# Two-layer hybrid decoder trunk: seven block products in the FFN's gate/up groups, and other step tables at the DeltaNet's edges

## The reference

```
h = h + gated_deltanet(rms_norm(h))       # layer 0: 16 q/k heads, 32 v heads of 128, chunks of 64
h = h + (silu(x @ Wg) * (x @ Wu)) @ Wd    # FFN, x = rms_norm(h), hidden width 5632
kv = shared_kv(rms_norm(h))               # projected, block-compressed once
h = h + nsa_attention(rms_norm(h), kv)    # layer 1
h = h + (silu(x @ Wg) * (x @ Wu)) @ Wd    # second FFN
out = rms_norm(h)
```

## Time and profile before

| | |
|---|---|
| runs | 2955.64, 2954.94, 2952.25 us, median 2954.94 |
| profiled execution | 2950.0 us, its span 2948.2 us |
| TensorE busy | 2823.6 us, 96%, 13696 matmuls |
| VectorE busy | 1800.2 us, 61% |
| ScalarE busy | 1497.7 us, 51% |
| DMA | 493.02 MB, mean 167 GB/s |
| granted TensorE clock | mean 0.986 of full |

### The profile page before, as it was taken

How to read it: one execution, slowest core, us unless ns; L and a number is a source line. 1 busy time by engine, 2 the same in 40 slices (tenths; PEclk the granted TensorE clock), 3 DMA queues, 4 the chain that set the end, 5 groups by cost and what they waited for, 6 DMA issues and landing times.

```text
span 2948.2 us, 39238 instructions
## 1 busy us (share of the span) xinstructions
PE 2823.6 (96%) x13696; PEld 2342.0 (79%) x13696; DVE 1800.2 (61%) x2183; ACT 1497.7 (51%) x1978; POOL 30.2 (1%) x29
## 2 busy tenths in 40 slices
PE   7989999999988999999999999799989999999997
PEld 6778887887866788888888878688878888888886
DVE  5767877877876555555555554556664555555555
ACT  6676767677664444444444444454444444444443
POOL 0000000000000000000000000000000000000000
PEclk9999999999998999999999999899999999999999
DMA  6434444444433555555555555533336555565553
GB/s 239 153 122 150 154 157 147 162 138 159 159 114 97 168 185 193 192 190 190 190 185 190 193 176 190 174 119 111 107 126 209 185 188 193 188 195 190 191 192 129
DMA packets 135079, 493.02 MB, mean 167 GB/s; under 512 B 15008, under 2 KB 15328, under 8 KB 134624
## 3 DMA queue, kind: packets, MB, share of 16 engines
q1 hardware_dynamic: 133776, 487.82, 50.1%
q10 hardware_dynamic: 1232, 4.23, 0.4%
HBM read 489.86 MB, written 2.13 MB: 167 GB/s over the span
## 4 chain that ended last, share of the span: by engine, by line
issue 56%; PE 40%; DVE 1%; DMA 1%; ACT 1%; POOL 0%; POOLq 0%; ACTq 0%; SPq 0%; DVEq 0%
PE ACC L527 12%; PE ACC L529 12%; PE ACC L528 12%; PE SIDE L535 1%; DMA RAW<-stream 1%; DVE W_LO L1258 1%; PE SIDE L854 0%; PE SIDE L828 0%; ACT W_HI L909 0%; PE SIDE L851 0%; PE SIDE L833 0%; PE SIDE L838 0%; PE SIDE L866 0%; DVE H L1283 0%; ACT WORK L914 0%
## 5 line engine op out<-in xcount | busy, mean ns | idle before, releaser
L1258 DVE TENSOR_TENSOR W_LO<-RAW,W_HI 128x1024 fp32r<-128x1024 f32 x912 | 1100.5, 1222 | 767.9 <-ACT W_HI L909 764.2
L909 ACT ACTIVATE W_HI<-RAW 128x1024 fp32r<-128x1024 f32 x912 | 959.7, 1059 | 1008.0 <-PE ACC L529 983.4
L527 PE MATMUL ACC<-W_HI,X_HI 128*128 128x512 f32 x2496 | 990.2, 397 | 16.9 <-DVE W_LO L1258 12.5
L528 PE MATMUL ACC<-W_LO,X_HI 128*128 128x512 f32 x2496 | 975.7, 391 | 0.0
L529 PE MATMUL ACC<-W_HI,X_LO 128*128 128x512 f32 x2496 | 975.5, 391 | 0.0
L527 PEld LDWEIGHTS ACC<-W_HI,X_HI 128*128 128x128 f32 x2496 | 471.2, 189 | 112.1 <-issue 18.0
L529 PEld LDWEIGHTS ACC<-W_HI,X_LO 128*128 128x128 f32 x2496 | 470.7, 189 | 99.7
L528 PEld LDWEIGHTS ACC<-W_LO,X_HI 128*128 128x128 f32 x2496 | 471.4, 189 | 93.0 <-issue 0.5
L527 PE MATMUL ACC<-W_HI,A_HI 128*128 128x512 f32 x1024 | 410.2, 401 | 13.1 <-issue 10.4
L529 PE MATMUL ACC<-W_HI,A_LO 128*128 128x512 f32 x1024 | 403.0, 394 | 0.0
L528 PE MATMUL ACC<-W_LO,A_HI 128*128 128x512 f32 x1024 | 402.3, 393 | 0.0
(11 more groups left out here) (247 smaller groups left out, 1688.8 us busy)
## 6 DMA issues: line engine op xcount, KB each, us to landing
RAW<-stream SPq DMA_DIRECT2D x912, 512.0 KB, 3.9
WORK<-gdn_rows ACTq DMA_DIRECT2D x8, 512.0 KB, 4.2
WORK<-xt SPq DMA_DIRECT2D x4, 512.0 KB, 9.3
H<-x SPq DMA_DIRECT2D x2, 1024.0 KB, 13.3
out<-WORK SPq DMA_DIRECT2D x4, 512.0 KB, 3.9
WORK<-tails SPq DMA_DIRECT2D x2, 512.0 KB, 11.1
WORK<-gfin SPq DMA_DIRECT2D x1, 1024.0 KB, 8.3
K<-consts SPq DMA_DIRECT2D x1, 518.0 KB, 6.7
```

The source lines that it names most:

```text
L527: nc.tensor.matmul(dst, hi[:, at:at + P], wh, start=first and h % 2 == 0 and q == 0, stop=False)
L528: nc.tensor.matmul(dst, hi[:, at:at + P], wl, start=False, stop=False)
L909: nc.scalar.activation(W_HI[:, h % WS, :], raw_piece(h), ACT.Copy).then_inc(hi_ready, 1)
L1258: nc.vector.tensor_tensor(W_LO[:, h % WS, :], raw_piece(h), W_HI[:, h % WS, :].bitcast(f32), SUB).then_inc(lo_ready, 1)
```

## The change

**FFN.** In groups 1 to 10, half of the contraction of gate and up (every other pair of 128-row blocks) goes by a Strassen-Winograd scheme: with tokens in two blocks and columns in two, seven block products of sums take the place of eight. In each quarter j of a group six operations follow one another: `11`, `21`, `13`, `24` (the seven products), `pa`, `pb` (the other pair of blocks, ordinarily). `21` is half as wide. `13` and `24` multiply sums of weight blocks, which VectorE forms from RAW (`weight_sum`: t13 of 1024, t24 in two halves) and which are then split like a piece; they come from no DMA. Sums of token blocks are formed once per FFN (`token_sums`). A column group holds 256 columns each of gate and up. Four products go to the ACC tiles and are mixed by VectorE (`c_add`), the rest are accumulated in SIDE; `c_sum` adds both up. The transposes of the hidden activations stand before the last two down pieces, go through a copy in SBUF (`hid_t`), and A_HI and A_LO are made from that. Group 10 is written out beside the loop. SP frees RAW by a list (`RAW_FREE`).

**DeltaNet.** Iterations 0, 1, 7, 8 and 9 get piece lists of their own; four output pieces move from 7 to 8 (`old4` to `old7`). Tables for 0, 1, 7 and 8 and the one of the loop are new. Accumulators alternate over the written-out iterations. The activations of group 6 go to another buffer, B_HI and B_LO.

```diff
+FFN_PIECE = {"11": 0, "21": 1, "13": 0, "24": 0, "pa": 2, "pb": 3}
+FFN_ORDER = 4 * ["11 21 13 24 pa pb"]
+FFN_OPS = [(kind, j, 4 * j + FFN_PIECE[kind]) for j in range(4) for kind in FFN_ORDER[j].split()] +     [("d", n, 16 + n) for n in range(8)]
+FFN_AT = {op[:2]: e for e, op in enumerate(FFN_OPS)}
+RAW_FREE = [FFN_AT[kind, j] for j in range(4) for kind in ("11", "21", "pa", "pb")] + [24 + n for n in range(8)]
+MORE = 8 * (FBLK - 1)
...
+PIECES_0 = "qk 0 1 2 3 4 6 7 8 v 9 10 11 12 13 14 15 16 z 17 18 20 21 23 25 27 29"
+PIECES_1 = "qk 0 1 2 3 4 5 6 7 v 8 9 10 11 12 13 14 15 z 16 18 20 22 25 28 29 30"
+PIECES_7 = "qk 0 1 2 3 4 5 6 7 v 8 9 10 11 12 13 14 16 out 18 20 25 30"
+PIECES_8 = "old4 0 1 2 3 z 4 5 6 8 9 10 11 12 out 13 14 15 16 18 19 20 26"
+PIECES_9 = "out 0 1 2 3 4 5 6 7"
...
+def gdn_accs():
+    accs, turn = {}, 0
+    for it in sorted(GDN_PIECES):
+        slots = gdn_slots(it)
+        if it == LATE_Z:
+            turn = 0
+        for part, n in (slots[hs] for hs in sorted(slots)):
+            if n == 0 or (part in ("out", "old") and n % 2 == 0):
+                turn = 1 - turn
+            accs[it, part, n] = turn
+    return accs
...
 LAST_STEPS = gdn_table(SOLVE, """
-    0 y0
-    1 t0 u0
-    2 conv_v0a y1
-    3 t1 u1 conv_v0b
-    4 y2 strict
-    5 t2 u2 conv_v1a
-    7 y3
-    8 t3 u3 conv_v1b silu_v y4
+    0 y0 t0 u0 conv_v0a
+    2 y1 t1 u1 conv_v0b
+    3 y2 strict
+    4 t2 u2 conv_v1a
+    6 y3
+    7 t3 u3 conv_v1b silu_v
+    8 y4
     9 t4 u4
-    10 y5 v_t2
-    11 t5 u5
-    12 nw
+    10 v_t2 y5
+    11 t5
+    12 u5 nw
     13 ru
-    14 v0
-    15 s ks
+    14 v0 s
+    15 ks
     16 v1 o
-    19 osum oscale
+    18 osum oscale
     20 o_t""")
...
 FIRST_STEPS = gdn_table(ONCE, """
     8 gates1
     10 gates1b
     13 gates2""") + gdn_table(PREP, """
-    9 qk_t conv_qk0a conv_qk0b
-    10 conv_qk1a
+    8 qk_t conv_qk0a conv_qk0b
+    9 conv_qk1a
     11 conv_qk1b
-    15 silu_qk squares
-    17 ss fill qkn factors
-    20 k_t dif v_t
-    21 beta decay kkqk qk1 nr init masks""")
+    12 silu_qk
+    14 squares
+    17 ss fill factors qkn
+    20 v_t dif k_t
+    21 beta kkqk decay
+    22 qk1 nr init
+    23 masks""")
...
+        def gdn_act(g):
+            return (B_HI, B_LO) if isinstance(g, int) and g == GROUPS - 2 else (A_HI, A_LO)
...
+        def three(dst, hi, lo, wh, wl, start, stop):
+            nc.tensor.matmul(dst, hi, wh, start=start, stop=False)
+            nc.tensor.matmul(dst, hi, wl, start=False, stop=False)
+            return nc.tensor.matmul(dst, lo, wh, start=False, stop=stop)
+        def up_products(pe, c, e):
+            kind, j, _ = FFN_OPS[e]
+            pe.wait_ge(lo_ready, c + (e + 1))
+            m1, m6, m7, m5 = (ACC[i][:, k * COLS:(k + 1) * COLS] for i in range(2) for k in range(2))
+            c11, c12, c21, c22 = (SIDE[1 - i][:, k * COLS:(k + 1) * COLS] for i in range(2) for k in range(2))
+            kt = 4 * j + (2 if kind[0] == "p" else 0)
+            a11, a21, a12, a22 = (tuple(b[:, at:at + P] for b in (X_HI, X_LO))
+                                  for at in ((kt + q) * SEQ + t * P for q in range(2) for t in range(NT)))
+            z5, z7, z6, z3 = (tuple(b[i][:, k * COLS + j * P:k * COLS + (j + 1) * P] for b in (Z_HI, Z_LO))
+                              for i in range(2) for k in range(2))
+            f, l = j == 0, j == 3
+            early = f and FFN_AT["pa", 0] < FFN_AT["24", 0]
+            todo = {"11": [(m1, a11, 0, f, l), (c12, z3, 1, f, False)],
+                    "21": [(c11, a12, 0, f, False)],
+                    "13": [(m5, z5, 0, f, l), (m7, z7, 1, f, l)],
+                    "24": [(m6, z6, 0, f, l), (c21, a22, 1, f and not early, False)],
+                    "pa": [(c11, a11, 0, False, False), (c21, a21, 0, early, False), (c12, a12, 1, False, False),
+                           (c22, a22, 1, f, False)],
+                    "pb": [(c12, a11, 0, False, l), (c22, a21, 0, False, l), (c11, a12, 1, False, l),
+                           (c21, a22, 1, False, l)]}[kind]
+            for dst, (hi, lo), half, start, stop in todo:
+                wh, wl = (b[:, e % WS, half * COLS:(half + 1) * COLS] for b in (W_HI, W_LO))
+                m = three(dst, hi, lo, wh, wl, start, stop)
+            m.then_inc(w_used, 1)
...
+            for e in range(0 if first or final_ else 24):
+                if e == 0:
+                    pe.wait_ge(acc_out[0], ph.before("m16", it))
+                if e == FFN_AT["24", 0] or FFN_OPS[e][0] == "pa" and e < FFN_AT["24", 0]:
+                    pe.wait_ge(side_out[0], ph.before("hid_t", it))
+                if e == FFN_AT["13", 0]:
+                    pe.wait_ge(acc_out[1], ph.before("m57", it))
+                up_products(pe, c, e)
+            for k in range(0 if first else 4):
+                pe.wait_ge(acc_out[k % 2], ph.before(f"down{k}", it))
+                if k == 0:
+                    pe.wait_ge(act_lo, it + (FBLK if ph is FFN1 else 0))
+                if k == 3 and not final_:
+                    pe.wait_ge(hid_done, it + (FBLK - 1 if ph is FFN1 else 0))
+                    turn(by_block(hid), 0)
+                for half in range(2):
...
+        def ffn_hi(act, ph, base, ob, it, e):
+            (kind, j, piece), wrap = ffn_ahead(it, e)
+            act.wait_ge(w_used, ffn_c(ob, it) + (e + 1 - WS))
+            dst = W_HI[:, e % WS, :]
+            if kind in ("13", "24"):
+                act.wait_ge(t_done, sums_done(ph, it, wrap) + (3 * j + (1 if kind == "13" else 3)))
+                src = t13 if kind == "13" else t24
+            else:
+                act.wait_ge(raw_full[piece % RAWS], (ffn_raw(base, it) + 24 * wrap) * (16 // RAWS) + 16 * (piece // RAWS + 1))
+                src = raw_piece(piece)
+                if kind == "21":
+                    dst, src = dst[:, 0:COLS], src[:, COLS:2 * COLS]
+            nc.scalar.activation(dst, src, ACT.Copy).then_inc(hi_ready, 1)
...
+                if k == 3 and not final_:
+                    take_out(act, 0, ph.after("hid_t", it), hid_t)
...
+                act.wait_ge(w_used, c + (16 if first else 32))
+                act.wait_ge(side_out[0], ph.after("hid_t", it))
+                nc.scalar.activation(A_HI[:, :], hid_t, ACT.Copy).then_inc(act_hi, 1)
...
+        def ffn_lo(dve, ph, base, ob, it, e):
+            (kind, j, piece), wrap = ffn_ahead(it, e)
+            dve.wait_ge(hi_ready, ffn_c(ob, it) + (e + 1))
+            hi, lo = W_HI[:, e % WS, :].bitcast(f32), W_LO[:, e % WS, :]
+            if kind == "21":
+                nc.vector.tensor_tensor(lo[:, 0:COLS], raw_piece(piece)[:, COLS:2 * COLS], hi[:, 0:COLS],
+                                        SUB).then_inc(lo_ready, 1)
+            else:
+                src = {"13": t13, "24": t24}.get(kind, raw_piece(piece))
+                nc.vector.tensor_tensor(lo, src, hi, SUB).then_inc(lo_ready, 1)
+            for n in range(3):
+                weight_sum(dve, ph, base, ob, it, e + 2 - n, n)
+        def weight_sum(dve, ph, base, ob, it, e, n):
+            (kind, j, piece), wrap = ffn_ahead(it, e)
+            if kind != "11":
+                return
+            b11_22, b12_21 = raw_piece(piece), raw_piece(piece + 1)
+            done = sums_done(ph, it, wrap) + 3 * j
+            if n < 2:
+                dve.wait_ge(lo_ready, ffn_c(ob, it) + (e - 3 + n))
+            if n == 0:
+                for p in (piece, piece + 1):
+                    dve.wait_ge(raw_full[p % RAWS], (ffn_raw(base, it) + 24 * wrap) * (16 // RAWS) + 16 * (p // RAWS + 1))
+                i = nc.vector.tensor_tensor(tiles2(t13), tiles2(b11_22),
+                                            b12_21[:, 0:COLS].unsqueeze(1).broadcast_to([P, 2, COLS]), ADD)
+            else:
+                dve.wait_ge(t_done, done + n)
+                a = (t13 if n == 1 else t24)[:, 0:COLS]
+                b = (b11_22 if n == 1 else b12_21)[:, COLS:2 * COLS]
+                i = nc.vector.tensor_tensor(t24[:, (n - 1) * COLS:n * COLS], a, b, ADD)
+            i.then_inc(t_done, 1)
...
+            def hid_lo():
+                dve.wait_ge(act_hi, it + hi0)
+                nc.vector.tensor_tensor(A_LO[:, :], hid_t, A_HI[:, :].bitcast(f32), SUB).then_inc(act_lo, 1)
+            if final_:
+                hid_lo()
+            for e in range(0 if first or final_ else 24):
+                if e == 20:
+                    hid_lo()
+                if e == 22:
+                    dve.wait_ge(w_used, c + 22)
+                    dve.wait_ge(m1_out, it + late)
+                    nc.vector.tensor_tensor(dif, ACC[0][:, COLS:2 * COLS], c_add[:, 0:COLS], SUB).then_inc(acc_out[0], 1)
+                ffn_lo(dve, ph, base, ob, it, e + WS)
+                if e == 22:
+                    m7, m5 = ACC[1][:, 0:COLS], ACC[1][:, COLS:2 * COLS]
+                    dve.wait_ge(acc_out[0], ph.after("m16", it))
```

(25 more changed lines are left out.)

496 lines of the change are left out of this document (336 added, 160 removed).

## The result

The changed kernel takes 2915.03 us (median of 4 runs, 2910.82 to 2917.91) against 2953.6 for the kernel before beside it: ratio 0.9871, 95% interval 0.9853 to 0.9889. It is faster by 38.6 us where 84.7 was forecast, and it lies above the range, whose end was 2904. The direction was right, and the size less than half.

A forecast was written before the change was run, and what follows sets the result against it. TensorE, busy 2823.6 of 2948.2 us, was taken as the bound. Terms -54.3 + 2 - 2.8 - 11.6 - 18.0 = -84.7 us, from a median of 2954.94, gave 2870.2 us; range 2854 to 2904.

The forecast's parts named there:

- The failed step: FFN, t13's wait for raw 21: 4.7 to 6.2 us allowed, landing 3.5 to 5.4, so it fits; called most exposed.
- Rival C: FFN: t13 waits for raw 21 and stops VectorE and TensorE; decides from landings of 7.3 us, 3030 at 8.2; chance 0.04.
- -54.3 for 240 matmuls: Both FFNs: 12 fewer matmuls in each of 20 groups, at 0.2263 us each, save 54.3 us if TensorE stays the limit.
- VectorE, +2: FFN group starts, where slack is thinnest at 0.6 us: 0.1 us charged for each of 20 groups, bounds 0 to 20.
- rival A: FFN: VectorE, at 90% load, runs late and delays TensorE; half the FFN gain goes, 2897 us; chance 0.15.
- The last block, -2.8: End of each FFN: transposes before the last two products cut the wait from 4.9 to about 3.5; -2.8 us for both.
- Iterations 0 and 1, -11.6: First DeltaNet iterations: alternating accumulators and moved steps remove waits and half-rate loss, 14.6 us named, 3 given back.
- Iterations 2 to 6, 0: Middle DeltaNet iterations: a few steps move by a slot; no change expected, between -5 and +5 us.
- Iterations 7 to 9, -18.0: Last DeltaNet iterations: -8.5 idling in 8, -4.2 at the seam to 9, +2 in 7, -7.3 clock.
- This only moves work: Four output pieces, 10.9 us of products, go from DeltaNet iteration 7 to 8 with no gain or loss of their own.
- About 5.5 of idling in place of 14.0: DeltaNet iteration 8: changed waits, with direct steps y1 to t1 and y0 to t0 at 1.7 us each, give -8.5 us.
- -7.3 for the clock: DeltaNet iterations 7 to 9: of about 11 us lost at half rate, two thirds go with the waits.

The follow-up runs named there:

- t13 later: Changed kernel with VectorE's weight sum t13 issued one place later, behind the low part of pb instead of ahead of it: 2884.55 us.
- the run with the operation inside the loop: Kernel with t13 later plus one useless 512-wide VectorE operation per quarter, ahead of the low part of 21: 2887.89 us.
- The run that took it away: Kernel with t13 later, ks moved to slot 21 in iteration 1 and a piece between ks and v1 in iterations 1 and 7: 2885.71 us.
- the one without the wait: Changed kernel with t13 and t24 formed from raw piece pb, so no early wait for raw 21; part of the computation left out: 2885.38 us.

## Why the prediction was wrong in size

**The failed step, 32 us by the stages and 30.5 by the medians: "4.7 to 6.2 us. Landing takes 3.5 to 5.4, median 3.9. It fits".** The places were laid out rightly, the comparison was wrong. The allowance of 6.2 is had once: a t13 that starts late also frees raw 21 late. What must fit into every turn is all that lies between two t13s: 5.3 us of VectorE, 0.2 to ask, the landing, 0.1 to start. At 10.2 that leaves 4.6 for a landing, and 3.9 is a median of requests spread evenly. Bunched as the new order bunches them they take 5.5. The prediction named this wait as the one most exposed and noted that pieces would be asked for in pairs, but let only landings above 6.2 cost anything. Rival C had the right mechanism and a wrong point of decision: from 4.6 on it costs, not from 6.2.

**-54.3 for 240 matmuls.** Held but for 8 us: with no wait left a group takes 63.9, not 63.5. In a steady group with t13 later (1141 to 1205 us) the matmuls that take a sum of token blocks, and those next to them, start 229 to 241 ns apart where others start 227 apart. That makes 0.37 of the 0.4; why they do isn't shown. Each FFN's first group takes 46.9 where it took 46.3. In all, the FFNs of the kernel with t13 later give 46.2 of the 55.1.

**VectorE, +2, and rival A.** VectorE's 56.7 us and its 1.14 from start to start held. That operations with a wait for VectorE's own result don't overlap was right in the rival, and costs 0.1: t13 and the first half of t24, neighbours once t13 is later, start 1.26 apart for a duration of 1.23 (1225.98 and 1227.24 in the run with the operation inside the loop). It never mattered. The +2 didn't come: with t13 later no steady group waits. The Trainium skill (VectorE: DVE Perf Modes, The DRAIN you can't avoid) lets the next operation start only when the pipe is empty, and excepts an operation that is not held, which the rival left out. The trace agrees with the exception, 1.14 apart where nothing is waited for; only the pair with a wait stands 1.26 apart.

**The last block, -2.8.** The wait came as forecast and the term was wrong. The wait stands at 3.63, beside 3.89 in the earlier trace rows, and the transposes' 1.0 is gone from it. But the transposes are TensorE's own work and only stand earlier now, ahead of two down pieces; they cost it their 0.8 to 1.0 there. What the change gives is 0.3 an FFN. (From group 10's first product to the shared K/V it is 98.0 us before and 95.4 with t13 later, and 2.3 of that is group 10's 12 matmuls. The second FFN's end gives 1.0 more, by a stretch at half rate of 3.4 us instead of 6.8.)

```profile
1673.60 0.47 PE L666 MATMUL ACC<-W_HI,A_HI 128*128 128x512 f32 x1 [3.63 <-issue]
```

**Iterations 0 and 1, -11.6.** Measured -12.2, in another split: 0 gave 11.5, its waits of 4.2, 2.8 and 1.4 and its half-rate stretches gone. Iteration 1 gave 0.7, because the 2.5 of ks to v1 replaced the seam's 2.8, and behind it stood 3.4 us at half rate that the kernel before didn't have there. I had priced such a direct pair in iteration 7 and not in 1. The run that took it away gained 3.0.

**Iterations 2 to 6, 0.** Measured -2.7, within the bounds of 5; what made it isn't shown.

**Iterations 7 to 9, -18.0, measured -3.8.** Three terms. "This only moves work" was the wrong one at the root: pieces in the edge iterations are cover, so taking four out of 7 raised its idling by 5.2, where I charged 2. "About 5.5 of idling in place of 14.0": the direct steps were priced one by one at 1.7, and y0 to t0 and y1 to t1 cost 1.7 and 1.9; but y3 waits behind two splits on ScalarE, and the chain y, t, u holds iteration 8 at 86 us with 16 pieces in it and at 88 to 89 with 20. 8 and the seam gave 7.5 of idling, not 12.7. And -7.3 for the clock: in the profiled execution the stretches at half rate stayed, 20.5 us of them against 23.9, worth 1.4. In the kernel with t13 later, the same program here, they were 6.8 us and TensorE was busy for 6.9 less than before, near the forecast; but its idling was then 27.6, above the 26.1 of before. Where the products went faster the waits were longer, and the sum was 209.7 us against 211.4. The seam to 9 itself went as forecast. The tables and the held back pieces only work together, which no sum of single prices could show.

## What to carry over

When a consumer is moved ahead in an in-order stream, don't ask whether its data land before they are wanted once; walk the cycle from its start to its next start through buffer release, request and landing, and compare that with the stage's period. Take the landing time at the spacing that the new order of instructions gives to the requests, and not the median of the kernel before: here 5.5 us and not 3.9. Work that fills gaps in a chain-bound stage can't be moved at no cost: price the stage it leaves and the one it enters by their chains, not by their products.

## What the runs showed of the hardware

In the FFNs a 512 KB piece lands in 3.4 to 3.6 us at the least, and in 5.5 on average when it is the last of three asked for within 3 us (changed kernel, and the one without the wait). The Trainium skill (DMA: Bandwidth & Descriptors, Anatomy of one DMA), for requests from GpSimd where these come from SP, gives a fixed 2.0 us plus the bytes at 436 GB/s, an estimate of 3.2, and has no term for other requests in flight. The measurement decides, and by it a loop of 5.6 plus 3.2 would have fitted into 10.2.

The granted clock differed between executions of the same DeltaNet instructions (iteration 7: 97.0 us at a mean of 0.95, 94.5 at 1.00). TensorE was busy for 84.3 and 80.3 us of them and idled for 12.7 and 14.2. That is 2.5 us that no change of the program made. Over iterations 7 to 9, the six executions of this program had 6.8 to 20.5 us at half rate.
